# Eight panel places for the S5 outputs instead of four, the first states ordered ahead of the last gate tiles, and two modulation pieces moved

## The chip, the cores and the metric

The kernel runs on one core of one Trainium2 chip. The metric is device time in microseconds (us) of one execution; the number compared is the median of several executions. All arithmetic is fp32, or fp32 split into two rounded halves (fp32r), so TensorE does the bulk of the work. The chip's DMA engines move weights and tables from HBM into SBUF.

## What is computed

The reference is two blocks of two layers each on 256 context and 256 latent tokens of width 1024. The change lies in the second layer of the first block, an S5 layer, and in the seam to the second block. Cut to what matters:

```python
mod = jax.nn.silu(c) @ ada_w[i] + ada_b[i]                  # "modulation": shift, scale, gate
h = x * (1.0 + scale) + shift
pz = h @ s5_w_in[0];  p, z = pz[..., :-E], pz[..., -E:]     # E = 2048
for rev in (0, 1):                                          # both directions
    abar, bbar, cmat = s5_discretise(...)                   # 128 groups of 16 channels, 64 states
    yc_dir, h_ctx = s5_scan(flip(uc), abar, bbar, cmat, 0)  # h[t] = abar h[t-1] + bbar u[t]; y = Re(cmat h)
    y_dir, _      = s5_scan(flip(u),  abar, bbar, cmat, h_ctx)
g = gelu(y);  y = g * sigmoid(g @ glu_w + glu_b)
x = layer_norm(alpha * x + gate * ((y * silu(z)) @ w_out[1]))
# second block: mod = silu(c_2) @ w_ada_2[l] + b_ada_2[l] (6 x 1024 columns), then rms_norm(x), attention, ...
```

## The kernel before

Every engine (SP for DMA issue, POOL, ACT, DVE, PE) runs its own straight program. One function `flow` (L1148, and for the S5 layer `S5.flow`, L1662) is written once and run for each engine, so the order of its lines is the order on every engine. Waits are on counted semaphores; an engine never passes an instruction that waits.

**Places for panels.** Weights and tables come in panels of 1 MB (2048 floats on each of 128 partitions). `WR_` is a `Ring` (L128) of four such places in `wbuf`. `take` hands out the next place and makes SP wait until the last reader of what lies there is done. SP is in order, so a panel whose place isn't free holds back all panels behind it.

**The S5 layer.** The scan is done in blocks of 8 tokens. The states between blocks run through a recurrence of 62 steps for each half of the groups (`recur_dve`, L1518: four DVE instructions for a step). The half `hf` = 0 is early; half 1 starts when the last inputs have entered (a point with the mark "in"). TensorE does meanwhile the gate projection `z` in 16 tiles of 128 columns, half of them between the inputs and the last eight behind them (`rest(z)`). `before_act` (L1534) copies the states of one half into the order in which the outputs read them: two large copies after step 46, then copies for each of two quarters after step 62; `before_dve` (L1548) does a part of half 1.

**The outputs.** They come in four quarters q = 0 to 3; quarters 0 and 1 read half 0, quarters 2 and 3 read half 1. `leave_pe` (L1598) does for each quarter two accumulations ("y", q, 0) and ("y", q, 1) of 48 matmuls each. The trace counts each fp32 matmul as two instructions, so one is x96 there. Each accumulation needs three panels: one Toeplitz panel (`ttab`, kind "t") and two output panels (`ctab`, kind "c"), the second "c" panel only from its middle on. After both, the result is copied (`rows_to`, L1632), turned by eight transposes (line L122) and passed through gelu on ACT. I number the 24 panels n = 6 q + 0 ... 5, in the order t0, c0, c1, t1, c2, c3. `panels_sp` (L1578) issues them; `panel_ring` (L1570) says where each goes. Panels 0 to 11 and 16 to 23 go to the four places of `WR_`. Panels 12 to 15 go to `WX`, four places in the memory of the states of half 0, free once ("y", 1, 1) is done.

**Modulation pieces.** `backlog` is a chain of pieces (class `Ada`, L584), each a 1 MB panel of `w_ada`, 8 matmuls (x16 in the trace), an ACT copy to `mrow`, and 2 small matmuls with 2 ACT instructions that turn the row. A piece normally turns the row of the piece before it; pieces 7 and 11 of a chain ("flush") turn their own as well. `step(backlog, n)` puts n pieces at a place of the program. In the kernel before, pieces 8 and 9 of the second block's first chain stand between quarters 1 and 2, and pieces 10 and 11, then 12 to 16, stand inside the layer norm LN2 (L668) after the S5 layer:

```python
            ln = on(LN2)
            step(ln)
            step(backlog, 2)
            step(ln)
            step(backlog, 5)
            e.mark("ctx2")
```

`Ctx2` (L1088) then makes SP wait for the mark "ctx2", the end of all of these on every engine, before it loads the second context over the buffers that LN2 used. The S5 layer ends with the mark "s5"; the halves of g (`HalvesG`, L1069), the GLU's matmuls, the second output projection and LN2 follow.

Of the kernel before, what the change touches and what calls it, by code (L numbers as in the profile page):

```python
# [164 lines left out]
def step(gen, n=1):  # L165
    for _ in range(n):
        next(gen, None)


def rest(gen):  # L170
    for _ in gen:
        pass


def chain(*gens):
    for g in gens:
        yield from g


def build(nc, I, out):  # L180
    ctx = ExitStack()
    with ctx:
        def sb(name, n):
            return ctx.enter_context(nc.sbuf_tensor(name, [128, n], F32))
# [48 lines left out]
        A = sb("A", AN)  # L233
# [914 lines left out]
        def flow(e, on):  # L1148

            on(Load())  # L1150
            on(TurnIn())
            ada0, setup = on(ADA[0]), on(SS.setup)
            step(setup)
            step(ada0, 3)
            step(setup)
            step(ada0, 2)
            step(setup)
            step(ada0, 3)
            e.mark("mod1")
            on(Mod1())  # L1160
            for v in VTM:
                on(v)
            proj, backlog, tables = on(PROJ1), chain(ada0, *[on(a) for a in ADA[1:]]), on(SS.tables)
            setup = on(SS.setup2)
            for i in range(24):
                step(proj)
                step(setup)
                if i in (14, 19, 21, 23):
                    step(tables)
            on(PowersStored())  # L1170
            at = 0
            for g in range(4):
                for i, _ in enumerate(on(AT1[g])):
                    if i < 16 and g < 3:
                        step(proj)
                    elif g < 3 or i % 3 == 0:
                        step(backlog)
                    if g == 3 and i % 4 == 3 and i < 16:
                        SS.part(e, "toeplitz", i // 4)
                    if at % 7 in (0, 2, 4, 5):  # L1180
                        step(tables)
                    at += 1
                if g == 2:
                    rest(tables)
                    on(TablesDone(SS))
            e.mark("at1")
            outp = on(OUT1)
            on(HalvesOO())
            for i, _ in enumerate(outp):
                if i in (1, 3, 5):  # L1190
                    SS.part(e, "toeplitz", 4 + i // 2)
            ln = on(LN1)
            step(ln)
            step(backlog, 4)
            step(ln)
            step(backlog, 4)
            e.mark("ln1")
            if e.name == "pool":
                SS.stacks(e)
            on(Mod2())  # L1200
            SS.flow(e, on, backlog)
            e.mark("s5")
            on(HalvesG())
            rest(on(GLU))
            if e.name == "dve":
                e.wait_ge(act_evac, ("ada1", "M"))
            rest(on(OUT2))
            ln = on(LN2)
            step(ln)
            step(backlog, 2)  # L1210
            step(ln)
            step(backlog, 5)
            e.mark("ctx2")
            on(Ctx2())
            for L in LAYERS:
                L.flow(e, on, backlog)
            e.mark("end")
            on(FIN)
            e.mark("last")

        def sp_program(sp):
            flow(sp, lambda st: st.sp(sp) if hasattr(st, "sp") else iter(()))

        def pool_program(pool):
            flow(pool, lambda st: st.pool(pool) if hasattr(st, "pool") else iter(()))

        def act_program(act):
            flow(act, lambda st: st.act(act) if hasattr(st, "act") else iter(()))
# [39 lines left out]
class S5:  # L1268
# [5 lines left out]
    def __init__(self, nc, I, L):  # L1274
# [46 lines left out]
        self.S = [A[:, a:a + 8192].rearrange("p (s r g) -> p s r g", s=64, r=2) for a in (18176, 26368)]  # L1321
        self.WX = self.ring([A[:, 18176 + 2048 * i:20224 + 2048 * i] for i in range(4)])
        self.landed_x = [sig(f"landed_x{i}") for i in range(4)]
        self.G = A[:, 4864:8960].rearrange("p (k t) -> p k t", k=16)
        self.YC = A[:, 8960:9984].rearrange("p (t x m) -> p t x m", t=8, x=8)
        self.PTS = [X[:, 4 * i:4 * i + 4, 0:256].rearrange("p (k a) (s c) -> p k a s c", k=2, s=4) for i in range(2)]
# [242 lines left out]

    def panel_ring(self, key):  # L1570
        q, kind, i = key
        n = self.panels(q).index(key) + 6 * (q - 2)
        return (self.WX, self.landed_x) if 0 <= n < 4 else (self.WR_, self.landed_w)

    def panel(self, key):
        return self.panel_ring(key)[0][key]

    def panels_sp(self, sp, q):  # L1578
        if q == 0:
            sp.wait_ge(self.l_tt, 7)  # L1580
            sp.wait_ge(self.l_ct[0], 30)
            sp.wait_ge(self.l_ct[1], 31)
        for key in self.panels(q):
            r, sems = self.panel_ring(key)
            if r is self.WX:
                sp.wait_ge(self.mm_done, ("y", 1, 1))
            _, kind, i = key
            last = (self.mm_done, ("y", q, i if kind == "t" else i // 2))
            s = r.take(sp, key, last)
            sem = sems[r.of[key]]  # L1590
            if kind == "c":
                sp.dma(s.rearrange("p (j f) -> p j f", j=4),
                       self.ctab.rearrange("p (q j x) f -> p q j (x f)", q=4, j=4)[:, q, :, 512 * i:512 * i + 512]
                       ).then_inc(sem, key)
            else:
                sp.dma(s, self.ttab[2 * q + i]).then_inc(sem, key)
# [65 lines left out]
    def flow(self, e, on, backlog):  # L1662
        def part(name, *a):
            self.part(e, name, *a)
# [57 lines left out]
            u += 2  # L1722
        e.mark("in")
        part("recur", 1)
        rest(z)
        part("before", 0)
        for q in range(2):
            part("panels", q)
            part("leave", q)
        step(backlog, 2)  # L1730
        part("panels", 2)
        part("panels", 3)
        part("before", 1)
# [1269 lines left out]
```

## Time and profile before

| | us |
|---|---|
| median of 3 runs | 2534.68 (2533.98 to 2544.1) |
| profiled execution, its own time | 2543.55 |
| its span in the trace | 2541.7 |
| PE busy in the span | 2211.3 (87%) |
| DVE busy | 1337.6 (53%) |
| ACT busy | 906.5 (36%) |
| POOL busy | 443.0 (17%) |

The span runs from the first to the last instruction; the execution's own time is 1.85 us longer. Times in the trace count from the span's start. The mean granted clock of TensorE was 0.921 of full speed (1.0 is 2.4 GHz, 0.5 is 1.2 GHz). Shares of busy time are means over stages with different limits, so the stage itself has to be read: quarters 0 to 3 lie at about 965 to 1050 us, LN2 at 1206 to 1230 us.

### The profile page before, as it was taken

To read this page: it belongs to the slowest core of one execution; us is meant where nothing else is said; L and a number is where in the kernel's file an instruction comes from. 1 tells how busy PE (TensorE), PEld (TensorE's weight loads), DVE (VectorE), ACT (ScalarE), POOL (GpSimd) and SP (SyncE) were. 2 spreads that over 40 slices of the span, in tenths; PEclk is the share of its full clock that TensorE was granted. 3 is DMA by queue.
4 is the path that set the end of the run, shared out by engine and by line. 5 is a ranking of instruction groups with operands and counts; after the bars stand their busy time and mean duration, and the time that the engine had idled before them with its cause. 6 is when DMAs were issued, how large, how long until landed. Compare 5 with 4: busy or idle time off the path is not lost.

```text
span 2541.7 us, 33862 instructions
## 1 busy us (share of the span) xinstructions
PE 2211.3 (87%) x13593; PEld 1672.4 (66%) x13593; DVE 1337.6 (53%) x2599; ACT 906.5 (36%) x1779; POOL 443.0 (17%) x417
## 2 busy tenths in 40 slices
PE   6979798879989995699898976889999997878998
PEld 5757576647546694599463433678888764547997
DVE  4648686565479847364425356443333244455554
ACT  3234454552222363353222444232222212444443
POOL 0047878509821000000000000000000000000000
PEclk8979898989999997899899987989999998978999
DMA  8154444685687646865621212322323422224653
GB/s 285 65 183 129 143 144 111 189 258 166 204 267 229 203 150 246 285 183 164 198 68 50 86 48 84 126 89 84 99 84 94 121 83 83 83 83 135 197 161 105
DMA packets 434035, 366.34 MB, mean 144 GB/s; under 512 B 66238, under 2 KB 412622, under 8 KB 431702
## 3 DMA queue, kind: packets, MB, share of 16 engines
q1 hardware_dynamic: 392212, 320.87, 40.9%
q0 software_dynamic: 7424, 26.38, 2.8%
q10 hardware_dynamic: 34242, 16.92, 2.3%
q8 instruction: 108, 1.77, 0.3%
q14 instruction: 49, 0.40, 0.1%
HBM read 317.58 MB, written 54.92 MB: 147 GB/s over the span
## 4 chain that ended last, share of the span: by engine, by line
PE 69%; DVE 14%; DMA 6%; ACT 6%; POOL 3%; issue 2%; ACTq 1%; SPq 0%; DVEq 0%; POOLq 0%
PE ps L119 66%; DVE A L88 3%; PE ps L122 3%; ACT A L115 3%; POOL A L88 3%; DVE R L88 2%; DVE A L102 2%; DMA wbuf<-ctab 2%; DVE A L92 1%; DVE A L105 1%; DVE A L93 1%; DMA wbuf<-in_ada_w 1%; DMA A<-btab 1%; DVE A L96 1%; ACT A L116 1%
## 5 line engine op out<-in xcount | busy, mean ns | idle before, releaser
L119 PE MATMUL ps<-R,R 128*128 128x256 f32 (+1 forms) x3968 | 849.0, 336 | 33.5 <-ACT R L115 23.4
L119 PEld LDWEIGHTS ps<-R,R 128*128 128x128 f32 x3968 | 634.7, 194 | 108.1 <-ACT R L115 28.6
L119 PE MATMUL ps<-HR,R 128*128 128x512 f32 (+1 forms) x1984 | 557.8, 365 | 35.4 <-DVE R L88 24.8
L88 DVE TENSOR_TENSOR R<-wbuf,R 128x1024 fp32r<-128x1024 f32 (+2 forms) x304 | 349.5, 1158 | 368.0 <-ACT R L115 367.8
L119 PEld LDWEIGHTS ps<-HR,R 128*128 128x128 f32 x1984 | 358.9, 194 | 94.7 <-issue 28.5
L115 ACT ACTIVATE A<-ps 128x512 f32<-128x512 f32 (+4 forms) x400 | 210.3, 556 | 583.9 <-PE ps L119 419.3
L115 ACT ACTIVATE R<-wbuf 128x1024 fp32r<-128x1024 f32 (+2 forms) x304 | 270.1, 894 | 293.6 <-PE ps L119 266.9
L88 DVE TENSOR_TENSOR A<-A 128x128 f32<-128x128 f32 (+4 forms) x868 | 320.6, 400 | 88.1 <-ACT A L115 58.6
L119 PE MATMUL ps<-H,wbuf 128*128 128x512 f32 (+2 forms) x928 | 336.6, 520 | 13.8 <-DVE H L93 13.8
L119 PE MATMUL ps<-A 128*128 128x64 f32 (+10 forms) x1736 | 290.0, 369 | 33.3 <-DVE A L88 7.6
L88 POOL TENSOR_TENSOR A<-A 128x512 f32<-128x512 f32 (+3 forms) x186 | 215.4, 1170 | 528.2 <-DVE A L96 268.4
L119 PEld LDWEIGHTS ps<-H,wbuf 128*128 128x128 f32 (+1 forms) x928 | 176.5, 193 | 159.8 <-issue 134.5
L119 PEld LDWEIGHTS ps<-A 128*128 128x128 f32 (+3 forms) x1736 | 187.8, 191 | 86.8 <-issue 41.5
L88 POOL TENSOR_TENSOR A<-X 128x576 f32<-128x576 f32 x128 | 168.4, 1336 | 102.3 <-ACT X L115 75.4
L122 PE MATMUL ps<-C,A 128*128 128x128 f32 (+1 forms) x663 | 101.9, 295 | 65.5 <-DVE A L92 29.3
L125 POOL DMA_DIRECT2D A<-in_rope x3 | 1.8, 598 | 876.9 <-DVE X L96 471.8
L122 PEld LDWEIGHTS ps<-C,A 128*128 128x128 f32 (+1 forms) x663 | 81.5, 153 | 109.9 <-issue 62.1
L119 PE MATMUL ps<-A,C 128*128 128x256 f32 (+5 forms) x296 | 105.4, 507 | 53.3 <-ACT A L115 52.5
L88 DVE TENSOR_TENSOR A<-ps,A 128x256 f32<-128x256 f32 (+1 forms) x100 | 53.5, 535 | 135.1 <-PE ps L119 133.2
L115 ACT ACTIVATE R<-A 128x256 fp32r<-128x256 f32 (+1 forms) x108 | 50.1, 502 | 170.0 <-DVE A L88 169.6
L119 PEld LDWEIGHTS ps<-A,C 128*128 128x128 f32 (+2 forms) x296 | 44.0, 185 | 101.0 <-ACT A L115 54.7
L102 DVE RECIPROCAL A<-A 128x1 f32<-128x1 f32 (+4 forms) x120 | 98.4, 820 | 16.7 <-ACT A L115 14.1
(103 smaller groups left out, 1644.0 us busy)
## 6 DMA issues: line engine op xcount, KB each, us to landing
wbuf<-in_w_ada SPq DMA_DIRECT2D x48, 1024.0 KB, 5.2
wbuf<-in_ada_w SPq DMA_DIRECT2D x24, 1024.0 KB, 8.5
wbuf<-in_w_out SPq DMA_DIRECT2D x24, 1024.0 KB, 5.7
wbuf<-in_w_ffn_gate SPq DMA_DIRECT2D x22, 1024.0 KB, 5.3
wbuf<-in_w_ffn_up SPq DMA_DIRECT2D x22, 1024.0 KB, 5.7
wbuf<-in_w_ffn_down SPq DMA_DIRECT2D x32, 704.0 KB, 4.7
wbuf<-in_attn_w_in SPq DMA_DIRECT2D x20, 1024.0 KB, 7.0
ctab<-A ACTq DMA_DIRECT2D x64, 256.0 KB, 2.8
```

Source lines behind the costliest of these rows:

```text
L88: return self.op(lambda e: e.tensor_tensor(out, a, b, op))
L92: return self.op(lambda e: e.tensor_scalar(out, a, s1, None, op0))
L93: return self.op(lambda e: e.tensor_scalar(out, a, s1, s2, op0, op1))
L96: return self.op(lambda e: e.scalar_tensor_tensor(out=out, in0=a, scalar=s, in1=b, op0=op0, op1=op1))
L102: return self.op(lambda e: e.reciprocal(out, a))
L105: return self.op(lambda e: e.reduce_max(out, a, AX_X))
L115: return self.op(lambda e: e.activation(out, a, func, bias=bias, scale=scale))
L116: return self.op(lambda e: e.activation(out, a, func, bias=bias, scale=scale, accum_out=accum))
L119: return self.op(lambda e: e.matmul(out, lhsT, rhs, start=start, stop=stop, skip_group_check=True))
L122: return self.op(lambda e: e.transpose(out, a, ident))
L125: return self.op(lambda e: e.dma_start(dst, src, allow_slow_non_contiguous=slow), 16)
```

## The change

Three things are changed.

The places of the panels: one place `WG` for panels 0 and 8, one place `WB` for panels 1, 9 and 20, two places `WH` for panels 6, 7, 14 and 15 in the memory of H (the layer's input, free once the last tile of z is done), and `WX` now takes panels 16 to 19. The other eleven (2 to 5, 10 to 13, 21 to 23) stay in `WR_`. `WG` and `WB` lie in buffers of the input stage, so SP waits for the mark "in" first.

The order: `part("before", 0)`, which is ACT's ordering copies for half 0, stands ahead of `rest(z)`, the last eight gate tiles.

The modulation pieces: no pieces between quarters 1 and 2; seven instead of five in the second place of LN2. So pieces 8 and 9 now stand in LN2's first place, and pieces 10 to 16 in its second.

```diff
@@ flow
             ln = on(LN2)
             step(ln)
             step(backlog, 2)
             step(ln)
-            step(backlog, 5)
+            step(backlog, 7)
             e.mark("ctx2")
@@ S5.__init__
+        hf = self.H.rearrange("p k t -> p (k t)")
+        self.WG, self.WB = self.ring([A[:, 6912:8960]]), self.ring([A[:, 9984:12032]])
+        self.WH = self.ring([hf[:, 0:2048], hf[:, 2048:4096]])
+        self.landed_g, self.landed_b = [sig("landed_panel_g")], [sig("landed_panel_b")]
+        self.landed_h = [sig(f"landed_panel_h{i}") for i in range(2)]
@@ S5.panel_ring
-        n = self.panels(q).index(key) + 6 * (q - 2)
-        return (self.WX, self.landed_x) if 0 <= n < 4 else (self.WR_, self.landed_w)
+        n = self.panels(q).index(key) + 6 * q
+        for ns, r in (((0, 8), (self.WG, self.landed_g)), ((1, 9, 20), (self.WB, self.landed_b)),
+                      ((6, 7, 14, 15), (self.WH, self.landed_h)), ((16, 17, 18, 19), (self.WX, self.landed_x))):
+            if n in ns:
+                return r
+        return self.WR_, self.landed_w
@@ S5.panels_sp
         if q == 0:
+            sp.wait_mark("in")
             sp.wait_ge(self.l_tt, 7)
...
             if r is self.WX:
                 sp.wait_ge(self.mm_done, ("y", 1, 1))
+            if r is self.WH:
+                sp.wait_ge(self.mm_done, ("z2", 1920))
@@ S5.flow
         e.mark("in")
         part("recur", 1)
+        part("before", 0)
         rest(z)
-        part("before", 0)
         for q in range(2):
             part("panels", q)
             part("leave", q)
-        step(backlog, 2)
         part("panels", 2)
         part("panels", 3)
         part("before", 1)
```

How this moves instructions on three engines follows; lines with - stand only in the kernel before, lines with + only in the changed one.

On SP, from the last gate panels on (`in_s_w_in` is the gate's weights; `wbuf` is `WR_`, `A` holds `WG`, `WB` and `WX`, `H` holds `WH`):

```order
 L125 DMA wbuf<-in_s_w_in 128x8x256 x3
+L125 DMA A<-ttab 128x2048
+L125 DMA A<-ctab 128x4x512
+L125 DMA wbuf<-ctab 128x4x512
 L125 DMA wbuf<-ttab 128x2048
 L125 DMA wbuf<-ctab 128x4x512 x2
-L125 DMA wbuf<-ttab 128x2048
-L125 DMA wbuf<-ctab 128x4x512 x2
-L125 DMA wbuf<-ttab 128x2048
-L125 DMA wbuf<-ctab 128x4x512 x2
-L125 DMA wbuf<-ttab 128x2048
-L125 DMA wbuf<-ctab 128x4x512 x2
```

The order of the panels is the same, but their places are no longer all in `wbuf`.

On ACT, at the end of the gate and through the quarters (`A<-ps 128x256 x8` are the last eight gate tiles, `A<-A` the ordering copies, `128x8x64` the quarters' results, `128x4x128` the gelu):

```order
-L115 ACTIVATE A<-ps 128x256 x8
 L115 ACTIVATE A<-A 64x2048
 L115 ACTIVATE A<-A 64x1920
 L115 ACTIVATE A<-A 64x32x32 x4
+L115 ACTIVATE A<-ps 128x256 x8
 L115 ACTIVATE A<-ps 128x8x64 x2
 L115 ACT_TABLE_LOAD
@@ -566,6 +566,4 @@
 L115 ACTIVATE A<-ps 128x8x64 x2
 L115 ACTIVATE A<-ps 128x4x128 x2
-L115 ACTIVATE mrow<-ps 128x256 x2
-L115 ACTIVATE MOD<-ps,VT 128x2 x2
```

The six copies of half 0 now precede the gate's evacuations, and the modulation's ACT work no longer precedes the copies of half 1.

On PE, in LN2 (`ps<-X,C` is its mean, `ps<-A,C` its sum of squares, `wbuf,CS` the matmuls of modulation pieces, `C,mrow` their turns):

```order
 L119 MATMUL ps<-X,C 128x256 x8
+L119 MATMUL ps<-wbuf,CS 32x256 x16
+L119 MATMUL ps<-C,mrow 128x2 x2
+L119 MATMUL ps<-A,C 128x256 x8
 L119 MATMUL ps<-wbuf,CS 32x256 x8
 L119 MATMUL ps<-C,mrow 128x2 x2
 L119 MATMUL ps<-wbuf,CS 32x256 x8
 L119 MATMUL ps<-C,mrow 128x2 x4
-L119 MATMUL ps<-A,C 128x256 x8
```

Pieces 8 and 9, with a single turn, take the place ahead of the sum of squares, and pieces 10 and 11 move behind it.

## Rows read from the trace of the kernel before

**Rows 1.** The page of the whole execution: its span.

```profile
span 2541.7 us, 33862 instructions
```

**Rows 2.** Chain of waits, 925 to 1065 us: start, us, what.

```profile
930.77 34.67 PE ps L119 x176
...
971.68 4.80 PE ps L119 x96
...
987.00 5.42 DMA wbuf<-ctab
...
1010.39 16.73 DMA wbuf<-ctab
...
1044.43 4.34 PE ps L119 x96
...
1059.60 5.49 PE ps L119 x26
```

**Rows 3.** Timeline, 935 to 1034 us: start, us, engine, line, operation [idle before <-releaser].

```profile
935.99 4.26 ACT L115 ACTIVATE A<-ps 64x512 f32<-64x512 f32 x6 [1.35 <-PE ps L119]
...
940.28 65.43 DVE L88 TENSOR_TENSOR A<-A 128x128 f32<-128x128 f32 x248 [32.90 <-ACT A L115]
...
965.74 8.05 ACT L115 ACTIVATE A<-A 64x2048 f32<-64x2048 f32 x6
...
995.15 1.73 PEld L119 LDWEIGHTS ps<-wbuf,A 128*32 128x32 f32 x48 [0.40 <-DMA wbuf<-ctab]
...
1005.75 1.29 DVE L99 COPY A<-A 64x1024 f32<-64x1024 f32 x2
...
1015.24 5.76 ACT L115 ACTIVATE A<-A 64x2048 f32<-64x2048 f32 x4
...
1020.10 4.44 PE L119 MATMUL ps<-A 128*32 128x128 f32 x96 [5.21 <-ACT A L115]
...
1032.38 1.09 PE L122 MATMUL ps<-C,A 128*128 128x128 f32 x8 [0.82 <-DVE A L99]
```

**Rows 4.** Timeline of SP's DMA queue, 965 to 1008 us.

```profile
965.45 0.33 SPq L125 DMA_DIRECT2D wbuf<-ttab  x1
...
998.15 9.53 SPq L125 DMA_DIRECT2D wbuf<-in_w_ada  x2
```

**Rows 5.** Engines by stretch: length, busy (instructions) each, clock, DMA share, GB/s.

```profile
930.00:965.00 35.00, 35.00 (x183) 31.33 (x181) 23.13 (x95) 10.84 (x21) 0.00 (x0) 1.00 0.36 121
...
987.00:1007.30 20.30, 10.36 (x200) 8.89 (x200) 18.81 (x74) 4.49 (x5) 0.00 (x0) 0.75 0.88 312
1010.00:1031.00 21.00, 10.56 (x204) 8.78 (x204) 0.69 (x1) 7.29 (x9) 0.00 (x0) 0.67 1.04 399
```

**Rows 6.** PE alone by stretch: length, busy (instructions), granted clock, DMA share, GB/s.

```profile
1020.00:1024.60 4.60, 4.44 (x96) 0.62 1.01 395
1035.00:1036.60 1.60, 1.52 (x48) 1.00 1.12 444
```

**Rows 7.** Timeline of PE in LN2, 1212 to 1229 us.

```profile
1212.43 1.18 PE L119 MATMUL ps<-C,mrow 128*128 128x2 f32 x8
1214.42 6.25 PE L119 MATMUL ps<-A,C 128*128 128x256 f32 x16 [0.81 <-ACT A L115]
...
1223.00 1.07 PE L119 MATMUL ps<-wbuf,CS 128*32 128x256 f32 x16
...
1224.53 1.07 PE L119 MATMUL ps<-wbuf,CS 128*32 128x256 f32 x16
...
1227.09 1.07 PE L119 MATMUL ps<-wbuf,CS 128*32 128x256 f32 x16 [0.95 <-DMA wbuf<-in_w_ada]
```

**Rows 8.** Timeline of SP's DMA queue in LN2, last modulation panel.

```profile
1221.73 0.37 SPq L125 DMA_DIRECT2D wbuf<-in_w_ada  x1
```

**Rows 9.** Chain of waits, end of LN2: start, us, what.

```profile
1229.41 0.42 DVE X L93
...
1229.97 5.00 DMA A<-in_ctx
```


## The prediction

> **What bounds the kernel now.** I read the page for the span [rows 1], then the chain of waits over the stretch that the change touches [rows 2], then the timelines of the engines and of SP there [rows 3, 4], then the granted clock and the DMA rate by stretch [rows 5, 6], and at last LN2 [rows 7 to 9]. In the chain the reader is to see four kinds of link. First, PE until 965.44 with the last gate tiles, then 6.2 us of ACT until quarter 0 starts at 971.68 [rows 2]: ACT evacuates the last tile and only then makes the ordering copies of half 0, 8.05 us for six [rows 3]. Second, waits for `ctab` panels through quarters 0 and 1 (987.00 for 5.42 us is one) [rows 2]. Third, a stop before quarter 2: it starts at 1020.10, released by ACT [rows 3]. Fourth, panels again: a 16.73 us transfer in quarter 2, and the last accumulation at 1044.43 [rows 2]. It ends at 1048.77; the GLU runs steadily from 1059.60 [rows 2].
>
> The view that decides is DVE's row: the recurrence of half 1 begins at 940.28 and runs 65.43 us, to 1005.7, and the copies behind it take until 1007.04 [rows 3]. Quarters 0 and 1 need none of it, quarters 2 and 3 all of it. So whatever is gained before 1006.8 is only slack, and the stage can't end before 1006.8 plus quarters 2 and 3.
>
> **Part 1: first states ahead of the gate tiles.** ACT is free at 940.25 [rows 3], the states of half 0 have been ready longer, so the copies run 940.3 to 948.3. The gate tiles' evacuations wait up to 7 us. Two or three of eight banks are held by that, and PE doesn't stop. Quarter 0 then starts at about 965.5 instead of 971.7. By itself that is worth 0: DVE's recurrence covers it, and without that cover it would be worth 6.2 us.
>
> **Part 2: places for panels.** I need the price of a transfer. A panel issued at 987.00 landed at 992.42, the one behind it by 995.15 [rows 2, 3]: 5.4 us for the first and 2.73 us for each that follows. The stretch with the deepest queue moved 399 GB/s at a DMA share of 1.04 [rows 5], or 2.63 us for 1.0486 MB. I take 2.75 us, with 2.6 and 2.95 as the ends; the pair of `ctab` panels is the nearest row. Then, by the new places: panels 0 and 1 go out at 940.3, 2 to 4 as the gate's panels come free, and 5, 6, 7 at 965.45, when the last tile is done (today only one panel goes out then [rows 4]). Panel 5 lands at 970.8. From here each accumulation frees places before the queue is empty, so the queue runs full: panel n lands at 970.8 + 2.75 (n - 5). Panel 8 comes at 979.0, 11 at 987.3, 14 at 995.5, 17 at 1003.8, 20 at 1012.0, 23 at 1020.3. Quarter 1 follows panel 11 and ends about 990, 17 us before it did. SP must not be late for this: panels 16 to 22 wait for ("y", 1, 1), about 990, while 12 to 15 are still on their way; 23 waits for ("y", 2, 0), about 1011, with 20 to 22 still ahead.
>
> **Part 3: no pieces between quarters 1 and 2.** Today SP issues their two panels in 9.53 us from 998.15 [rows 4], PE and ACT work on them, and ACT reaches the copies of half 1 at 1015.24 only. They take 5.76 us for four; half 0's six took 8.05 [rows 3], so a small one takes (8.05 - 5.76) / 2 = 1.15 us and the two large ones (which need step 46 alone) some 3.5. Now ACT makes the large two right after quarter 1's gelu, at about 993, and one small one after 1005.7. Quarter 2 starts at 1006.85, which is 13.25 us earlier than 1020.10.
>
> **Quarters 2 and 3.** An accumulation takes 4.44 us where TensorE starts at the lower clock (granted 0.62 in that stretch), and half of one takes 1.52 us at a granted 1.00, so a whole one 3.1 us [rows 6]. PE is idle from 992 to 1006.85, so the first costs 4.44. The second follows at once, and I take 3.1. The turn between the quarters costs 0.82 us of waiting for the copy and 1.1 us [rows 3]. The last two take 3.1 each. The sum is 15.7, giving 1022.5. Panel 23 (1020.3, needed for the last half, 1.55 us) gives 1021.9, so the two limits lie together; with 0.2 for links the end is 1022.7. Today it is 1048.77: **gain 26.1 us**, half of it from the earlier start. Bounds: if three accumulations behind the first run at the lower clock, 19.3 us, end 1026.1, gain 22.7; if all run at the higher, end 1021.2, gain 27.6.
>
> The Trainium skill (DMA: Bandwidth & Descriptors, section Where 436 GB/s comes from) says that for transfers between HBM and SBUF the HBM side binds, at about 358 GB/s. By that a panel costs 2.93 us and the end would be near 1025.5. The trace here doesn't agree: 399 GB/s over 21 us [rows 5].
>
> What follows the last accumulation, 10.83 us to the GLU's steady run [rows 2], is the same chain of copy, gelu, halves. The GLU's first panel is issued behind panel 23 and lands near 1025, before the halves are done. GLU and second projection are PE's own pace behind that and move as a block.
>
> **Part 4: two more pieces in LN2.** Today pieces 10 and 11 stand ahead of the sum of squares, which starts at 1214.42; piece 11 is a flush, its four small matmuls take 1.18 us instead of 0.6 [rows 7] with two ACT instructions more. With 8 and 9 there I count 0.9 us less. Behind the sum, a piece takes 1.53 us on PE (1223.00 to 1224.53), and the last waited for its panel [rows 7]: issued at 1221.73 [rows 8], used at 1227.09, 5.3 us. All this ends under DVE's normalisation, which ends at 1229.83 and releases the load of the context at 1229.97 [rows 9]. Now four panels (8 to 11) are resident when LN2 begins, 12 and 13 go out when 8 and 9 are done, and 14, 15, 16 only when 10, 11, 12 are done, behind the sum. In the old times less 0.9: piece 10's matmuls end at 1220.7, 11's at 1222.2, 12's at 1224.4. Panel 14 lands at 1226.0, 15 at 1228.8, 16 at 1231.6. Piece 16 ends on ACT at 1233.7 instead of everything at 1229.9: **loss 3.8 us**. Nothing covers it, as SP's load of the context is queued behind that mark and PE waits for it. Bounds: 2 us if panels overlap more, 8.5 us if each of the three takes its full 5.3 us behind the other. `Ctx2` and all behind it see the same pieces done, so nothing else changes. The added waits on SP cost nothing: the mark "in" is set at 940.3, SP's earlier loads are issued by then, and the next panel couldn't go out before today either.
>
> **The sum.** -26.1 + 3.8 = -22.3 us. The profiled execution took 2543.55 (its span is 2541.7 [rows 1]), so its like would take 2521.3. The median of the runs shown lies 8.9 us lower, at 2534.68, and from it the forecast is **2512.4 us**.
>
> **Rivals.**
> - A. The memory limit holds over a queue of 55 us, longer than any today: a panel takes 2.93 us, the end is 1025.5, gain 23.3, net -19.5: 2515. For it: the deepest queue today lasts some 30 us only. Against it: 399 GB/s. Chance 0.10.
> - B. LN2 pays more: three panels of 5.3 us one behind the other, +8.5, net -17.6: 2517. For it: the wait at 1227.09 shows that this place is already short of panels. Against it: 2.73 us between two in a queue. Chance 0.12.
> - C. The change doesn't bring quarter 2 forward: some other wait of ACT, PE or SP holds it near 1020, and only the panels' waits inside quarters 2 and 3 go, 12.9 us, less 3.8: net -9, 2525.5. Against it: I find nothing between gelu of quarter 1 (993) and the copies. Chance 0.05.
> - D. Slower: the recurrence, now the sole gate of quarter 2, is slowed by what is put beside it (ACT's ordering copies of the same memory, a DMA queue that is full throughout). It has 248 instructions of 264 ns start to start. It cancels the whole gain once it takes 22.3 us more, 354 ns each; at 400 ns it ends 34 us later, and the kernel is at 2546, +11.4. Against it: DVE's busy time was 243 ns for each instruction at a DMA share of 0.36 (23.13 us for 95) and 254 at 0.88 (18.81 for 74, which holds two large copies) [rows 5]. Chance 0.03.
>
> **How the numbers follow.** The forecast's own case (both terms within their bounds, 2508 to 2519) has 0.68, A 0.10, B 0.12, C 0.05, D 0.03, and 0.02 for something unseen. The range 2506 to 2522 holds the first three and takes in the scatter of the runs' median, and leaves out C, D and the ends of the noise. Faster by more than 0.5% (12.7 us, about what a measurement of this kernel can tell from no change): forecast, A and B, with a little lost to a slow median, 0.90. Within 0.5%: C and that loss, 0.07. Slower: 0.03.
>
> **What would show it.** Right: quarter 0 starts at 965.5 right behind the gate; quarter 1 ends near 990; PE then idles until DVE's recurrence ends and quarter 2 starts at about 1006.9; the last accumulation ends at 1022 to 1026; the GLU's steady run starts 23 to 27 us earlier; from the end of OUT2 to the context's load there are some 4 us more, with PE waiting for `in_w_ada` at the last two or three pieces. Wrong: quarter 2 released by ACT or by a panel; a stretch 965 to 1020 with DMA under 350 GB/s; DVE's recurrence longer than 66 us; LN2 longer by 8 us or by nothing.

## The result, and the profile after

| | before | changed |
|---|---|---|
| median, us | 2534.69 (2524.91 to 2544.1, 10 runs) | 2520.88 (2504.61 to 2533.38, 10 runs) |
| ratio | | 0.9931 (95%: 0.9909 to 0.9954) |
| span of the profiled execution | 2541.7 | 2502.8 |

The changed kernel is faster by 0.69% (0.46 to 0.91%) by the recorded ratio, which is about 17 us; the two medians differ by 13.8 us, or 0.54%. The interval holds both. A second set of runs of the same kernel (label `again`, below) gave 0.9928 (0.9900 to 0.9956), 19.9 us between medians. The two spans differ by 38.9 us, far more: so the first thing to do with the two traces is to cut them into what the change touches and what it doesn't.

I cut at two events. One is the start of the second half's recurrence, DVE's row of 65.4 us. The other is SP's load of the second context. Ahead of the first and behind the second the programs do the same work.

| part, us | before | changed | difference |
|---|---|---|---|
| start to recurrence | 940.28 | 931.93 | -8.4 |
| recurrence to context load (the stage) | 289.69 | 269.05 | **-20.6** |
| context load to end | 1311.7 | 1301.8 | -9.9 |

Only the middle row is the change's. The outer rows look like scatter, since one kernel shows it too: over the ten further traces of this study, whose programs are the same there or nearly so, the first is 933 to 942 us and the last 1302 to 1316. From here I give times within the stage, counted from the recurrence's start (931.93 in the trace after, 940.28 before), because there they repeat to 1 us in two traces of the changed kernel (269.05 and 269.69); of the kernel before there is one trace.

A little of the middle row is scatter as well. From the GLU's steady run to LN2's first matmuls (on X) every kernel here runs the same instructions on PE, and the twelve traces have 145.0 to 147.3 us for it: 146.75 before, 145.00 in the changed kernel, 145.10 in its second trace. So 1.7 us of the -20.6 can't be put down to the change.

Chain of waits of the changed kernel, around the quarters (start, us, what):

```profile
996.34 0.71 DVE A L88 x3
997.45 1.06 ACT A L115
998.56 7.15 PE ps L119 x192
1005.73 0.70 DVE A L99
1006.48 1.09 PE ps L122 x8
1007.57 3.61 PE ps L119 x122
1011.18 2.43 issue
1013.62 2.20 PE ps L119 x70
...
1026.58 18.49 PE ps L119 x142
```

The chain that ran through `ctab` transfers before [rows 2] holds none. It is DVE's recurrence, one ACT copy, and then PE from 998.56 on, with one stop of 2.43 us of kind "issue" inside the last accumulation. The GLU runs steadily from 1026.58, which is 94.65 behind the recurrence's start; before it was 119.32 [rows 2, 3].

Timeline of the changed kernel (start, us, engine, line, operation, idle before and releaser):

```profile
931.93 8.07 ACT L115 ACTIVATE A<-A 64x2048 f32<-64x2048 f32 x6
931.93 65.42 DVE L88 TENSOR_TENSOR A<-A 128x128 f32<-128x128 f32 x248 [32.91 <-ACT A L115]
...
957.00 1.74 PE L119 MATMUL ps<-A 128*32 128x128 f32 x56
...
968.90 3.22 PE L119 MATMUL ps<-H,A 128*32 128x128 f32 x56 [2.77 <-DMA H<-ctab]
...
980.87 0.60 ACT L115 ACTIVATE A<-ps 128x512 f32<-128x512 f32 x1 [5.95 <-PE ps L119]
...
984.26 3.73 ACT L115 ACTIVATE A<-A 64x2048 f32<-64x2048 f32 x2
...
997.45 2.00 ACT L115 ACTIVATE A<-A 64x1024 f32<-64x1024 f32 x2 [9.46 <-DVE A L88]
...
998.56 3.22 PE L119 MATMUL ps<-wbuf,A 128*32 128x128 f32 x56 [15.95 <-ACT A L115]
```

These answer to [rows 3]. ACT makes the six copies of half 0 at 931.93, alongside the gate tiles; quarter 0 starts at 957.00, or 25.07, with the last gate tile (before: 31.4). Quarter 1's second accumulation ends at 980.87, or 48.9 (before: 67.0). ACT then makes the two large copies of half 1 at 984.26, with nothing else in their way, and quarter 2 starts at 998.56, or 66.63, with 15.95 us of PE standing idle before it on ACT, who stands on DVE. Before it was 79.82.

SP and the DMA engines in the stage, as stretches (length, busy and instructions of PE, PEld, DVE, ACT, POOL, clock, DMA share, GB/s):

```profile
957.00:982.00 25.00, 15.60 (x397) 13.63 (x397) 23.39 (x96) 6.08 (x8) 0.00 (x0) 0.86 0.98 370
976.00:998.50 22.50, 4.13 (x104) 3.44 (x104) 21.09 (x83) 7.38 (x7) 0.00 (x0) 0.70 1.04 399
998.50:1003.50 5.00, 4.94 (x120) 4.68 (x124) 0.51 (x2) 0.96 (x2) 0.00 (x0) 0.65 1.04 405
```

From 959 to 1003.5 the queue never runs dry and moves 370 to 405 GB/s (before, [rows 5]: 312 over the 20 us to 1007.3, the end of the recurrence and of quarter 1).

PE in LN2, which answers to [rows 7 to 9]. The first of these lines is from the trace before, the others from the changed kernel:

```profile
1206.35 3.61 PE L119 MATMUL ps<-X,C 128*128 128x256 f32 x16
...
1171.58 3.61 PE L119 MATMUL ps<-X,C 128*128 128x256 f32 x16
...
1178.41 4.93 PE L119 MATMUL ps<-A,C 128*128 128x256 f32 x16 [0.81 <-ACT A L115]
1183.26 1.07 PE L119 MATMUL ps<-wbuf,CS 128*32 128x256 f32 x16
...
1189.53 1.07 PE L119 MATMUL ps<-wbuf,CS 128*32 128x256 f32 x16
...
1193.86 1.94 PE L119 MATMUL ps<-wbuf,CS 128*32 128x256 f32 x16 [2.72 <-DMA wbuf<-in_w_ada]
1195.72 1.01 PE L119 MATMUL ps<-C,mrow 128*128 128x2 f32 x4
1197.59 1.93 PE L119 MATMUL ps<-wbuf,CS 128*32 128x256 f32 x16 [0.85 <-DMA wbuf<-in_w_ada]
1199.45 1.01 PE L119 MATMUL ps<-C,mrow 128*128 128x2 f32 x4
```

The chain of waits there:

```profile
1188.05 9.49 DMA wbuf<-in_w_ada
...
1200.98 5.11 DMA A<-in_ctx
```

There are now two waits for a modulation panel (2.72 and 0.85 us; one of 0.95 before [rows 7]), and the two pieces behind them, 15 and 16, run at the lower clock (granted 0.50 from 1193.8 to 1201.0): 16 matmuls in 1.94 us instead of 1.07. From the GLU's steady run to the context's load it is 174.40 us; before it was 1229.97 - 1059.60 = 170.37 [rows 2, 9]. LN2 by itself, from its first matmuls on X to the context's load, grew by more: 1200.98 - 1171.58 = 29.40 us, and before 1229.97 - 1206.35 = 23.62. That is +5.8 us, and +5.4 in the second trace; the GLU stretch, 1.7 us shorter by scatter, hides the rest.

### The profile page after: what moved, and what is told of

It is laid out like the page before. It is cut to its first block, busy times and chain, and to the rows that moved or that the text cites. A ratio compares the mean times of both kernels' runs of the same rounds, so it can differ in the third digit from the quotient of the medians.

```text
span 2502.8 us, 33860 instructions
## 1 busy us (share of the span) xinstructions
PE 2184.6 (87%) x13593; PEld 1651.9 (66%) x13593; DVE 1338.9 (53%) x2599; ACT 906.5 (36%) x1779; POOL 443.3 (18%) x417
## 4 chain that ended last, share of the span: by engine, by line
PE 67%; DVE 17%; ACT 6%; DMA 5%; POOL 2%; issue 2%; ACTq 1%; SPq 0%; DVEq 0%; POOLq 0%
PE ps L119 64%; DVE A L88 6%; PE ps L122 3%; ACT A L115 3%; POOL A L88 2%; DVE R L88 2%; DVE A L102 2%; DVE A L92 1%; DVE A L105 1%; DVE A L93 1%; DMA wbuf<-in_ada_w 1%; DMA A<-btab 1%; DVE A L96 1%; ACT A L116 1%; ACT L115 1%
## 5 line engine op out<-in xcount | busy, mean ns | idle before, releaser
L119 PEld LDWEIGHTS ps<-HR,R 128*128 128x128 f32 x1984 | 355.3, 192 | 94.3 <-issue 28.4
L119 PE MATMUL ps<-H,wbuf 128*128 128x512 f32 (+2 forms) x928 | 338.1, 522 | 13.6 <-DVE H L93 13.5
L119 PE MATMUL ps<-A 128*128 128x64 f32 (+11 forms) x1896 | 289.4, 352 | 24.5 <-DVE A L88 7.7
L119 PEld LDWEIGHTS ps<-A 128*128 128x128 f32 (+5 forms) x1896 | 186.9, 181 | 77.4 <-issue 40.6
L122 PEld LDWEIGHTS ps<-C,A 128*128 128x128 f32 (+1 forms) x663 | 82.8, 154 | 109.2 <-issue 59.8
L119 PE MATMUL ps<-A,C 128*128 128x256 f32 (+5 forms) x296 | 102.1, 496 | 52.4 <-ACT A L115 51.4
L102 DVE RECIPROCAL A<-A 128x1 f32<-128x1 f32 (+4 forms) x120 | 98.4, 820 | 16.7 <-ACT A L115 14.2
L119 PEld LDWEIGHTS ps<-A,C 128*128 128x128 f32 (+2 forms) x296 | 42.3, 179 | 98.2 <-ACT A L115 52.7
```

The costliest lines, as they stand in the source:

```text
L102: return self.op(lambda e: e.reciprocal(out, a))
L119: return self.op(lambda e: e.matmul(out, lhsT, rhs, start=start, stop=stop, skip_group_check=True))
L122: return self.op(lambda e: e.transpose(out, a, ident))
```

## The experiments

Theory Q: once there are places, the DMA queue sets the end of quarter 3. Theory R: the recurrence is the gate. All runs are the changed kernel with one edit, except where said. The table gives, for each trace, times behind the recurrence's start: quarter 2's start, the end of the last accumulation, the GLU's steady run, the context's load. Two lengths follow: from the GLU to the context, and from LN2's first matmuls to the context ("LN2").

| kernel | Q2 start | last acc. | GLU | context | GLU to context | LN2 | median, us | ratio to before (95%) |
|---|---|---|---|---|---|---|---|---|
| before | 79.8 | 108.5 | 119.3 | 289.7 | 170.4 | 23.6 | | |
| changed | 66.6 | 83.9 | 94.7 | 269.1 | 174.4 | 29.4 | 2520.88 | 0.9931 (0.9909 to 0.9954) |
| again | 66.6 | 84.8 | 95.5 | 269.7 | 174.2 | 29.1 | 2519.42 | 0.9928 (0.9900 to 0.9956) |
| no_states | 66.6 | 84.6 | 95.3 | 268.8 | 173.5 | 28.4 | 2521.72 | 0.9936 (0.9916 to 0.9956) |
| no_places | 68.2 | 98.4 | 109.2 | 284.8 | 175.7 | 28.9 | 2536.65 | 0.9991 (0.9973 to 1.001) |
| pieces_back | 66.6 | 87.4 | 98.2 | 267.7 | 169.6 | 23.5 | 2517.37 | 0.9927 (0.9900 to 0.9953) |
| places_only | 66.6 | 91.5 | 102.3 | 272.8 | 170.5 | 23.4 | 2521.17 | 0.9933 (0.9918 to 0.9949) |
| half_rec | 57.7 | 82.9 | 93.6 | 268.2 | 174.6 | 29.6 | one run | |
| half_panels | 66.6 | 82.1 | 92.9 | 268.1 | 175.3 | 28.9 | one run | |
| half_both | 51.4 | 67.6 | 78.4 | 253.8 | 175.4 | 28.6 | one run | |
| pe_pad | 66.7 | 83.2 | 93.9 | 268.9 | 175.0 | 28.6 | one run | |
| ln2_places | 66.6 | 84.2 | 95.0 | 265.2 | 170.2 | 22.9 | 2510.92 | 0.9888 (0.9872 to 0.9904) |

**The same kernel again.** No edit.

> The changed kernel once more. Between the start of the second half's recurrence and the load of the second context its trace was 20.7 us shorter than before, yet the medians of ten runs differ by 13.8 only. Theory S (scatter ahead of and behind the stage hides it): the median comes out 18 to 23 us under before, ratio 0.991 to 0.993, and the stage in this trace is again 20 to 21.5 us shorter than in the trace of before. Theory G (something behind the stage gives 7 us back): the ratio stays at 0.9945 and the part behind the load of the context is longer than before by some 7 us.

Measured: stage 269.7 us, 20.0 less than before; ratio 0.9928; the part behind the context's load 1316.3 us in this trace against 1311.7 before. Theory S: the stage repeats and the ratio is in its range. The part behind was 1301.8 in one trace and 1316.3 in the other of one and the same kernel, so a loss of 7 us there can't be read from single traces either way; but over the eleven traces behind the change it is 1301.6 to 1316.3, on both sides of the 1311.7 before, which shows no sign of one. The 6 us between the two gains in the medians (13.8 and 19.9) are best put down to this scatter; that is argued, not shown.

**Without the new order of the first states** (`no_states`).

```diff
         part("recur", 1)
-        part("before", 0)
         rest(z)
+        part("before", 0)
```

> The change without its new order on ACT (first states again behind the last gate tiles). Theory Q (the DMA queue sets the end of quarter 3): quarter 0 starts 6.2 us later, panels 8 to 10 are asked for some 6 us later, when 5 to 7 have landed already, the queue stands still for 2 to 4 us and the end of quarter 3 moves by that: +2 to +4 us against the changed kernel in the stage. Theory R (the recurrence covers it, as the prediction said): 0. If neither covers it: +6.2.

Measured: the last accumulation ends at 84.6, as in the two traces of the changed kernel (83.9 and 84.8), and the stage is 268.8 us. The order of the first states is worth 0 here, as Theory R had it. SP's queue did stand open (panel 8 is asked for at 975.89, over 10 us behind panel 7 at 965.50), but it did not show:

```profile
1005.68 3.21 PE L119 MATMUL ps<-wbuf,A 128*32 128x128 f32 x56 [10.75 <-ACT A L115]
...
1019.42 1.91 PE L119 MATMUL ps<-wbuf,A 128*32 128x128 f32 x48 [1.52 <-DMA wbuf<-ctab]
1022.06 1.52 PE L119 MATMUL ps<-wbuf,A 128*32 128x128 f32 x48 [0.74 <-DMA wbuf<-ctab]
```

The last accumulation does wait for its panels now, 1.52 and 0.74 us, which it doesn't in the changed kernel; but it waits in the place of the "issue" stop of 2.43 us, and the two come out alike. So the 0 is partly luck: without that stop the changed kernel's last accumulation would have ended near 81.4, and this kernel, with its waits, would have been slower than it (an estimate, from 2.43 us taken off 83.9).

**Without the new places** (`no_places`): `panel_ring` as before, so 20 panels in the four places of `WR_` and panels 12 to 15 in `WX`.

> The change without its new places (first states early, no pieces between the quarters, old rings). Theory Q: quarter 1 ends near 997 in times of before instead of 990, panels 12 to 19 are asked for at once then and come every 2.75 us, quarter 2 waits for panel 14 at 1008, panels 20 to 23 wait for their places; the last accumulation ends near 1036, 12 us behind the changed kernel's. Against before that is 12 us less in the quarters and 4 more in LN2: -8 to -9 us. Rival (the gain of the change comes from the order and from the pieces alone): as fast as the changed kernel, quarter 3 ends within 3 us of it.

Measured: 98.4 for the last accumulation, 14.5 us behind the changed kernel; stage 284.8, 4.9 us under before; in the medians no difference from before that can be told (0.9973 to 1.001), and a clear one from the changed kernel. That is Theory Q, though less was left of the gain than it said (-8 to -9 us): LN2 lost 5 us, and the last accumulation came 2.5 us later than expected. The rows show who takes over:

```profile
1006.15 5.19 PE L119 MATMUL ps<-A 128*32 128x128 f32 x96 [6.53 <-ACT A L115]
1014.92 0.66 PE L119 MATMUL ps<-A 128*32 128x128 f32 x8 [3.58 <-DMA wbuf<-ctab]
...
1022.75 1.52 PE L119 MATMUL ps<-wbuf,A 128*32 128x128 f32 x48 [1.66 <-ACT A L115]
1025.32 1.52 PE L119 MATMUL ps<-wbuf,A 128*32 128x128 f32 x48 [1.05 <-DMA wbuf<-ctab]
1032.08 4.22 PE L119 MATMUL ps<-wbuf,A 128*32 128x128 f32 x96 [5.24 <-DMA wbuf<-ctab]
```

Quarter 2 starts at 1006.15, or 68.2: nearly on time even without the places. Then 3.58, 1.05 and 5.24 us of waits for `ctab`, much as before the change (2.71, 1.57, 1.08 and 5.28). So the order and the pieces bring the start forward by 11.6 us, and 10.1 us of that reach the last accumulation (98.4 against 108.5); LN2 takes 5.3 back. From quarter 2's start to the last accumulation it is 30.2 us without the places, 28.7 before and 17.2 in the changed kernel: the places are worth 14.5 us (13.6 against its second trace), more than half of the gain in the quarters.

**Pieces back between the quarters** (`pieces_back`).

```diff
-            step(backlog, 7)
+            step(backlog, 5)
...
             part("leave", q)
+        step(backlog, 2)
         part("panels", 2)
```

> The change with modulation pieces 8 and 9 back between quarters 1 and 2, the rest kept. Theory Q: quarter 2 still starts 1.1 us behind the recurrence, as quarter 1 has ended by 990 and ACT has 15 us for the two pieces; but their two panels stand in the queue ahead of panel 12, so the last accumulation ends 2 x 2.7 = 5.4 us later, and LN2 gives 4 us back: +1.4 us against the changed kernel (0 to +3). Rival (the pieces were what held quarter 2): quarter 2 starts 5 us or more behind the recurrence's end, +9 us in the quarters.

Measured: quarter 2 starts at 66.6, so the pieces don't hold it. The last accumulation ends 2.6 to 3.5 us later (not 5.4), and from GLU to context it is 169.6 instead of 174.4 (LN2 alone: 23.5 instead of 29.4 and 29.1). The stage is 267.7 us, 1.3 to 2.0 less than with the pieces moved, where I had expected 1.4 more: the two panels in the queue cost less than I thought. The medians, 2517.37 against 2520.88 and 2519.42, lie the same way but can't tell so little. Moving the pieces was not what freed quarter 2, and by these traces (one against two) it cost a little.

**The places alone** (`places_only`): both edits above together, so the kernel before with new places.

> The kernel before with the new places alone: first states behind the last gate tiles and pieces 8 and 9 between quarters 1 and 2, both as before. From the two single cuts (order of the first states 0, pieces back -1.3 to -2 us in the stage) it is as fast as the changed kernel or 1 to 2 us faster: stage 267 to 269 us from the recurrence's start to the context's load (before 289.7, changed 269.1). Rival (order and pieces have an effect only together, as quarter 1 ends 6 us later and then the pieces hold ACT): quarter 2 starts 3 to 6 us late, stage 271 to 275.

Measured: stage 272.8 us, within the rival's numbers but not by its mechanism: quarter 2 starts on time, at 66.6. What is late is the queue: panel 8 is asked for at 36.5 instead of 28.0 (969.65 - 933.12 and, in the changed kernel, 959.89 - 931.93), 8.6 us later, two modulation panels stand ahead of panel 12, and together these cost 7 us at the last accumulation, though the first alone cost 0 and the second alone 3:

```profile
1011.66 1.52 PE L119 MATMUL ps<-A 128*32 128x128 f32 x48 [1.88 <-DMA A<-ctab]
1014.25 1.52 PE L119 MATMUL ps<-A 128*32 128x128 f32 x48 [1.07 <-DMA A<-ctab]
1019.52 2.05 PE L119 MATMUL ps<-wbuf,A 128*32 128x128 f32 x48 [3.75 <-DMA wbuf<-ctab]
1022.32 2.19 PE L119 MATMUL ps<-wbuf,A 128*32 128x128 f32 x48 [0.74 <-DMA wbuf<-ctab]
```

Four waits for `ctab` in quarter 3, the longest 3.75 us. So the order of the first states has a worth after all, but only where the queue has no slack left.

**Halves.** In `half_rec` the second recurrence has 31 steps; in `half_panels` each panel's transfer is half as long; `half_both` has both.

```diff
-        for s in range(1, 63):
+        steps = range(1, 32 if hf else 63)
+        for s in steps:
...
-            dve.tt(S[:, s], S[:, s], TM[:, 1], ADD).then_inc(self.dve_step, ("rec", hf, s))
+            keys = [("rec", hf, s)] + ([("rec", hf, 46), ("rec", hf, 62)] if hf and s == 31 else [])
+            dve.tt(S[:, s], S[:, s], TM[:, 1], ADD).then_inc(self.dve_step, *keys)
```
```diff
-                sp.dma(s, self.ttab[2 * q + i]).then_inc(sem, key)
+                sp.dma(s[:, 0:1024], self.ttab[2 * q + i][:, 0:1024]).then_inc(sem, key)
```

(and the same for the output panels, columns 0 to 255 of each 512.)

> The changed kernel with 31 instead of 62 steps in the second half's recurrence (its last 31 states are left out, so the work of DVE is halved). Theory Q (the DMA queue alone sets the end of quarter 3): quarter 2 starts some 16 us earlier, but the last accumulation still ends 83 to 85 us behind the recurrence's start, as panel 23 comes no sooner: 0 to -1.5 us. Theory R (the recurrence is the sole gate): the last accumulation ends 10 to 16 us earlier.

> The changed kernel with every Toeplitz and output panel loaded only half (0.5 MB, the other half of each place keeps old values). Theory Q: what remains is PE's own pace behind the recurrence, 66.6 + 15.7 = 82.3 us, so the last accumulation ends 1.5 to 2.5 us earlier than the changed kernel's 83.9 to 84.8. If the queue were the sole limit: more than 10 us earlier. If the queue were no limit: 0.

> Both cuts together: 31 steps and half panels. If two limits lie side by side, either cut alone gives almost nothing and both give the full sum: quarters 0 to 3 follow each other at PE's pace, some 8 us each from 25 us behind the recurrence's start, and the last accumulation ends near 58 to 62 us, 22 to 26 us earlier. If only one of them is a limit, this run is no faster than the better of the two single cuts.

Measured: with half the recurrence quarter 2 starts 8.9 us earlier and the last accumulation ends 1.0 us earlier, because now two panels are waited for in quarter 3 (2.27 and 3.70 us for `ctab`, at 1011.08 and 1019.00); with half the panels it ends 1.8 us earlier; with both, 16.3 us. Two limits lie close together: to relieve one alone is worth less than 2 us, as the prediction had it. They are not quite level. The changed kernel waits for no panel in quarters 2 and 3, and of the 1.8 us with half panels 1.67 are a shorter "issue" stop (0.76 instead of 2.43, see `pe_pad`). So there the recurrence and PE's own pace set the end, and the queue would take over 1 us below. Of my numbers two missed: quarter 2 of `half_rec` started 8.9 and not 16 us earlier, and `half_both` ended at 67.6, not 58 to 62. The rows of `half_both` name a third limit behind the first two:

```profile
981.74 2.00 ACT L115 ACTIVATE A<-ps 128x512 f32<-128x512 f32 x2 [0.75 <-PE ps L122]
983.76 5.77 ACT L115 ACTIVATE A<-A 64x2048 f32<-64x2048 f32 x4
```

```profile
988.64 3.21 PE L119 MATMUL ps<-wbuf,A 128*32 128x128 f32 x56 [6.50 <-ACT A L115]
```

ACT's program has the copies of half 1 behind quarter 1's gelu (981.74). The four take 5.77 us, and PE stands 6.50 us for them. In `half_rec` PE stands the same 6.50 us before quarter 2, so this is also why its start moved by 8.9 and not by 16 us.

**The stop without a cause** (`pe_pad`). In the changed kernel PE stops inside the last accumulation, and the profile names nobody. In the second trace (`again`):

```profile
1009.88 2.83 PE L119 MATMUL ps<-A 128*32 128x128 f32 x96
1012.53 1.04 PE L119 MATMUL ps<-wbuf,A 128*32 128x128 f32 x26
1016.34 2.17 PE L119 MATMUL ps<-wbuf,A 128*32 128x128 f32 x70 [2.78 <-issue]
```

96 MATMULs are the third accumulation, then 26 of the last, then 2.78 us. It is at the same instruction in `after` (2.43) and `ln2_places` (2.87), and 0.76 in `half_panels`, where the panels have half the bytes. The edit moves PE's program against its data:

```diff
             p = self.PS.take(pe, ("y", q, xq), (self.dve_evac if hf else self.act_evac, ("y", q, xq)))
+            if q == 2 and xq == 0:
+                for _ in range(24):
+                    pe.mm(p[:, 0:128], self.ident, self.ident, True, True)
```

(with the wait for the states behind it.)

> The changed kernel with 24 idle fp32 matmuls (48 MATMUL instructions in the trace's count) put on PE between quarters 1 and 2, where it has nothing to do; their results are overwritten. In three traces PE stops for 2.4 to 2.9 us, for nothing that the profile shows, 26 MATMULs into the last accumulation; with half panels the stop at that instruction is 0.8 us. Theory L (the stop belongs to a place in PE's program, where the next block of instructions has to be loaded behind a full DMA queue): it now stands 48 MATMULs earlier, about 74 into the accumulation before. Theory W (it is a wait for panel 22 or 23 that the profile doesn't show): it stays 26 MATMULs into the last accumulation, or at its middle.

Measured:

```profile
1012.30 2.37 PE L119 MATMUL ps<-A 128*32 128x128 f32 x74
1015.63 0.75 PE L119 MATMUL ps<-A 128*32 128x128 f32 x19 [0.95 <-issue]
```

74 MATMULs into the accumulation before, to the instruction. So the stop belongs to a place in the program and not to a panel; it was 0.95 us long there. Panel 23 wasn't the cause in the changed kernel either: it was asked for near 1003.1 and landed 7.9 us later, near 1011.0, ahead of the stop.

What PE waits for does stand in the traces, among the DMA packets. Those that start between 1011.0 and 1011.2 in the changed kernel (queue and kind, packets, MB, share of 16 engines):

```profile
q1 hardware_dynamic: 110, 0.06, 115.4%
q8 instruction: 1, 0.02, 36.9%
```

One of them, of 16 KB, brings instructions. It runs from 1011.06 to 1012.25, and PE goes on at 1013.62, 1.37 us behind it. There are nine "issue" stops of PE in these quarters (one each in `after`, `again`, `ln2_places` and `pe_pad`, three in `half_panels`, two in `half_both`), and in all nine PE goes on 1.25 to 1.57 us after such a packet ended. The first two stops of `half_panels` have 128 MATMULs and 128 weight loads between them; the third comes 381 MATMULs on, with three packets for them. So the stop is the loading of the next block of instructions. Its length depends on when that packet starts: 0.1 us before PE stops to 0.3 us behind it in the three long stops (2.43, 2.78 and 2.87 us), 1.3 us or more before it in the six short ones (0.25 to 1.25 us). Why it started late in those three stays open. A full DMA queue doesn't explain it alone, as in `pe_pad` the DMA share over the 2 us before the stop was 1.07 to 1.21, and in the changed kernel 1.10 to 1.18.

**Places for LN2's panels** (`ln2_places`). Pieces 8 to 11 and 16 get four places in the memory of the GLU's halves (A, 12032 to 20224), free once the last GLU tile is done.

```diff
+        WE = ring([A[:, 12032 + 2048 * i:14080 + 2048 * i] for i in range(4)])
...
+            def place(self, i):
+                return (WE, landed_e) if self.name == "ada2" and 8 <= i < 12 or (self.name, i) == ("ada2", 16) else (WR_, landed_w)
...
+                    if (self.name, i) == ("ada2", 8):
+                        sp.wait_ge(mm_done, ("glu", 15))
```

> The changed kernel with five of the nine modulation panels of LN2 in the memory of the GLU's halves, which is free by then, so that all but one are resident before LN2. Theory P (LN2's 4 us are the wait for panels and the lower clock behind it): no wait for in_w_ada, from GLU's start to the context's load 170.5 to 171.5 us instead of 174.2 to 174.4, the stage 265 to 267 us, 2.5 to 3.5 us less than the changed kernel and 23 to 24 us less than before: ratio to before 0.990 to 0.992. Rival (the two pieces cost by their own work on PE and ACT): 173 us or more from GLU's start to the load, no gain.

Measured: 170.2 us from GLU to context, stage 265.2, ratio 0.9888 (0.9872 to 0.9904), median 2510.92. Theory P, slightly better than its range. The last pieces run one behind the other at the full clock (granted 1.00 from 1194.9 to 1202.0), without a wait, and LN2 takes 22.9 us instead of 29.4 and 29.1:

```profile
1194.91 1.93 PE L119 MATMUL ps<-wbuf,CS 128*32 128x256 f32 x32
...
1197.32 1.07 PE L119 MATMUL ps<-wbuf,CS 128*32 128x256 f32 x16
...
1198.85 1.07 PE L119 MATMUL ps<-wbuf,CS 128*32 128x256 f32 x16
...
1200.39 1.07 PE L119 MATMUL ps<-A,CS 128*32 128x256 f32 x16
...
1207.60 3.67 PE L122 MATMUL ps<-C,A 128*128 128x128 f32 x16 [5.60 <-DMA A<-in_ctx]
```

This version is 1.12% under before, where the change gives 0.69% and 0.72%. Its interval lies just below that of the first set of the change (0.9909 to 0.9954) and overlaps that of the second (0.9900 to 0.9956), so the runs make it likely, not certain, that it beats the changed kernel too; LN2's 6 us are clear in the trace.

## Why the prediction was right, and where its steps were not

The forecast was 2512.4 us, a ratio of 2512.4 / 2534.68 = 0.9912, just inside the measured interval (0.9909 to 0.9954); the median measured, 2520.88, is inside the range of 2506 to 2522, near its upper end, and its 13.8 us are 62% of the 22.3 forecast. Against the stage, where the two traces can be compared, -22.3 stands against -20.6 and -20.0. In its two terms: the quarters gained 24.7 and 23.8 us where 26.1 were forecast, and LN2 lost 5.8 and 5.4 where 3.8 were. That the sum came closer than its terms is the luck of a GLU stretch that was 1.7 us shorter in both traces.

- **The recurrence as the gate.** Right, and exact: quarter 2 was to start at 66.57 behind the recurrence's start, and started at 66.63.
- **Part 1, first states, worth 0 under the recurrence.** Right for the changed kernel (`no_states`), though partly because the panel waits that come without it fall into the "issue" stop. What the step left out is that it also frees panels' places 8.6 us earlier, which is worth 4 us at the last accumulation where the queue has no slack (`places_only` against `pieces_back`).
- **Part 2, the queue.** Right: panels arrive at 370 to 405 GB/s, quarter 1 ends at 48.9 (forecast 49.7), panel 23 lands near 79 (forecast 80.0), and without the places the last accumulation ends 14.5 us later.
- **Part 3, "no pieces between quarters 1 and 2" brings quarter 2 forward.** The start is right, the cause is not. With the pieces left where they were, quarter 2 starts at the same 66.6 (`pieces_back`). The places alone bring the start to 66.6 (`places_only`), the other two edits alone to 68.2 (`no_places`), where quarter 1 ends at 59.9; 13.25 us belonged to the change as a whole, and once the places are there this part adds nothing. Here the prediction counted ACT's delay of today as if it would last once quarter 1 ended 18 us earlier.
- **Quarters 2 and 3, 15.7 us.** Measured 17.3, and 18.2 in the second trace. The term that was mis-sized is the "0.2 for links": the stop of 2.43 us (2.78 in the second trace), the loading of a block of instructions, is in no term. Without it PE would have ended at 81.4, below the forecast 82.4, with panel 23 there. (The bound of 19.3 us takes some 4.3 us for each of the later accumulations; with the 4.44 named it is 19.7.)
- **Part 4, LN2, +3.8.** Right in mechanism: waits for panels 15 and 16. Mis-sized: LN2 itself grew by 5.8 and 5.4 us; the +4.0 and +3.8 from the GLU to the context look exact only by the scatter of the GLU stretch. The lower clock behind the waits was not in the sum. It makes the last piece, which nothing covers, take 1.94 + 1.01 us where 1.07 + 0.61 were priced, 1.3 us more and the larger part of what was missing. With the panels resident, neither the waits nor the lower clock appear and LN2 takes 22.9 us (`ln2_places`).
- **Rival A** (358 GB/s) is out: 399 GB/s over 22.5 us. The Trainium skill's figure (DMA: Bandwidth & Descriptors, Where 436 GB/s comes from) doesn't hold for this kernel on one core. **B**: LN2 lost 5.4 to 5.8, not 8.5. **C**: quarter 2 came forward. **D**: the recurrence took 65.42 us against 65.43, beside a full queue and ACT's copies.
- **The base.** I took the scatter of single runs as some 9 us; the ten runs of each kernel spread over 19 and 29 us, which is why a gain of 20 us in the stage shows as 13.8 in one set of medians and 19.9 in another.

## What to carry to other kernels

When two spans differ, cut both traces at events of the same work first, and compare only the part that the change touches: here 20 us of 38.9 were the change's. Give a gain to an edit only after undoing that edit alone: two edits can each be nearly enough for the same effect (the start of quarter 2), and two cuts can each be worth less than 2 us and together 16. When a stretch agrees with the forecast, split it once more: here LN2 was 1.7 us worse than it looked, behind a GLU stretch that was 1.7 us better. Work put "elsewhere" has its price in the new place; ask there which panels are resident when it begins, and what clock it runs at behind each wait.

## What the runs showed of the hardware that I had not expected

- PE can stop at a fixed place of its program, for 2.4 to 2.9 us in three traces and 0.3 to 1.3 us in six other stops; it is listed as "issue". Moving the program by 48 MATMULs moved the stop by 48, and each time a packet of 16 KB of kind "instruction" had ended 1.25 to 1.57 us before PE went on. The Trainium skill (Runtime: NRT & Kernel Launch, Instruction fetch mechanics) calls the cost of crossing a block of instructions mostly hidden; it wasn't hidden here.
- One core's load queue held 399 GB/s for over 20 us with 1 MB panels.
- DVE's chain of 248 dependent 128x128 instructions took 65.39 to 65.46 us in all nine traces that run it in full behind the change and 65.43 before, whatever ran beside it; the parts ahead and behind varied by 10 and 15 us.
